# One core, four layers: an opening in another order, and modulation rows that come back from DRAM as turned columns

## The reference, cut to what matters

```python
c_act = jax.nn.silu(c)
for l in range(2):
    mod = c_act @ ada_w[l] + ada_b[l]              # 1024 -> 6 x 1024
    shift_m, scale_m, gate_m, shift_f, scale_f, gate_f = jnp.split(mod, 6, axis=-1)
    h = rms_norm(x, g_pre_mix[l]) * (1.0 + scale_m) + shift_m
    proj = h @ w_in[l] + b_in[l]
    q, k, v, u = jnp.split(proj, ...)               # q, k rotated by position
    attn_out = sliding_window_attention_with_sinks(q, k, v, sinks[l])
    pool_out = causal_pool_mixer(u, pool_w[l], pool_scale[l])
    mix = jnp.concatenate([attn_out, pool_out], -1) @ w_out[l]
    x = x + gate_m * rms_norm(mix, g_post_mix[l])
    h = rms_norm(x, g_pre_ffn[l]) * (1.0 + scale_f) + shift_f
    f = (jax.nn.silu(h @ w_gate[l]) * (h @ w_up[l])) @ w_down[l]
    x = x + gate_f * rms_norm(f, g_post_ffn[l])
```

## Time and profile before

| what | value |
|---|---|
| median of three runs | 1180.57 us (1179.1 to 1184.54) |
| the profiled execution, whole | 1183.38 us |
| its span, first to last instruction | 1181.3 us, mean granted PE clock 0.996 |
| PE busy | 1145.1 us, 97% |
| DVE busy | 808.8 us, 68% |
| ACT busy | 632.7 us, 54% |
| POOL busy | 28.3 us, 2% |
| chain that ended last | PE 78%, DVE 10%, DMA 7%, ACT 4% |

### The profile page before, as it was taken

One profiled execution on the slowest core, in us unless ns is written; L12 is line 12 of the kernel. 1 busy time (PEld: TensorE's weight loads), 2 busy tenths in 40 slices (PEclk: granted clock), 3 DMA queues, 4 the chain that ended last, 5 costly groups with the idle time before them and its releaser, 6 DMA issues.

```text
span 1181.3 us, 19635 instructions
## 1 busy us (share of the span) xinstructions
PE 1145.1 (97%) x7899; PEld 1025.8 (87%) x7899; DVE 808.8 (68%) x1255; ACT 632.7 (54%) x1114; POOL 28.3 (2%) x61
## 2 busy tenths in 40 slices
PE   5899999999989999999999999999999999999997
PEld 3466999999878999999898899999989889999996
DVE  5697966798996855554677668566666866766663
ACT  3066533355556644444755766455455676555543
POOL 3100000000000000010000000000000000000000
PEclk9999999999999999999999999999999999999999
DMA  9994899998435575585343455555534435555530
GB/s 380 410 421 196 323 280 299 291 393 322 175 131 192 215 273 207 216 254 201 126 148 145 172 205 181 185 188 194 176 119 161 172 112 198 194 180 197 191 107 36
DMA packets 37305, 252.97 MB, mean 214 GB/s; under 512 B 4416, under 2 KB 4704, under 8 KB 8928
## 3 DMA queue, kind: packets, MB, share of 16 engines
q1 hardware_dynamic: 34992, 244.47, 58.0%
q0 software_dynamic: 2080, 7.25, 1.7%
q10 hardware_dynamic: 144, 0.00, 0.0%
HBM read 250.64 MB, written 1.06 MB: 213 GB/s over the span
## 4 chain that ended last, share of the span: by engine, by line
PE 78%; DVE 10%; DMA 7%; ACT 4%; issue 2%; SPq 0%; DVEq 0%; ACTq 0%
PE bank L490 22%; PE bank L492 22%; PE bank L491 22%; DMA raw_w<-weights 7%; DVE lo_w L1576 3%; DVE raw_w L1586 3%; PE bank L497 3%; PE bank L586 2%; PE bank L539 2%; ACT gtok L1139 1%; PE bank L629 1%; ACT hi_w L1134 1%; PE bank L929 1%; ACT prob L1252 0%; PE bank L689 0%
## 5 line engine op out<-in xcount | busy, mean ns | idle before, releaser
L1576 DVE TENSOR_TENSOR lo_w<-raw_w,hi_w 128x1024 fp32r<-128x1024 f32 (+3 forms) x346 | 409.0, 1209 | 124.6 <-ACT hi_w L1134 124.2
L1134 ACT ACTIVATE hi_w<-raw_w 128x1024 fp32r<-128x1024 f32 (+3 forms) x346 | 350.1, 1040 | 151.1 <-DMA raw_w<-weights 83.5
L490 PE MATMUL bank<-in_hi,lo_w 128*128 128x256 f32 x1408 | 395.9, 281 | 0.0
L492 PE MATMUL bank<-in_hi,hi_w 128*128 128x256 f32 x1408 | 393.2, 279 | 0.0
L491 PE MATMUL bank<-in_lo,hi_w 128*128 128x256 f32 x1408 | 393.1, 279 | 0.0
L490 PEld LDWEIGHTS bank<-in_hi,lo_w 128*128 128x128 f32 x1408 | 264.2, 188 | 2.5 <-issue 0.8
L491 PEld LDWEIGHTS bank<-in_lo,hi_w 128*128 128x128 f32 x1408 | 263.7, 187 | 1.9 <-issue 0.5
L492 PEld LDWEIGHTS bank<-in_hi,hi_w 128*128 128x128 f32 x1408 | 264.6, 188 | 0.0
L490 PE MATMUL bank<-hi_w,hid_lo 128*128 128x512 f32 x352 | 139.7, 397 | 1.3 <-DVE hid_lo L2059 1.0
L492 PE MATMUL bank<-hi_w,hid_hi 128*128 128x512 f32 x352 | 139.0, 395 | 0.0
L491 PE MATMUL bank<-lo_w,hid_hi 128*128 128x512 f32 x352 | 139.0, 395 | 0.0
(11 more groups left out here) (218 smaller groups left out, 1142.8 us busy)
## 6 DMA issues: line engine op xcount, KB each, us to landing
raw_w<-weights SPq DMA_DIRECT2D x215, 1024.0 KB, 5.3
ink<-ink_w SPq DMA_DIRECT2D x8, 640.0 KB, 13.1
rows<-norm_rows POOLq DMA_DIRECT2D x5, 512.0 KB, 4.9
ink<-whole_w SPq DMA_DIRECT2D x2, 1024.0 KB, 23.5
early_out<-whole_w SPq DMA_DIRECT2D x2, 1024.0 KB, 12.8
rows<-mod_rows POOLq DMA_DIRECT2D x4, 512.0 KB, 9.1
raw_w<-weights SPq DMA_DIRECT2D x2, 832.0 KB, 4.4
const<-const_table SPq DMA_DIRECT2D x1, 1538.0 KB, 7.8
```

Source lines behind the costliest of these rows:

```text
L490: nc.tensor.matmul(o, st[1], mv[0], start=start, stop=False, **kw)
L492: return nc.tensor.matmul(o, st[0], mv[0], start=False, stop=stop, **kw)
L1134: nc.scalar.activation(hi_w[:, m % NSPLIT, cut], raw_view(unit)[:, cut], ACT.Identity).then_inc(*sig("hi_w", unit, i))
L1576: nc.vector.tensor_tensor(lo_w[:, m % NSPLIT, cut], raw_view(unit)[:, cut], hi_w[:, m % NSPLIT, cut].bitcast(F32), ALU.subtract).then_inc( ...
```

## The change

The opening sends c as one row of 4 KB ahead of x, and PE spreads it into two banks, from which ACT takes silu. The squares of T1 go to DVE, the norms stand ahead of the first `ada` products, T1's norm has a buffer of its own (`gained`), and the first two units come in halves. One of three ACT table loads on the way is gone.

`turn_column` turns a column `modcol` of 128 x 8 by one PE transpose into 8 x 128; `piece` on ACT copies that to `pieces`, and `row_out` writes it as 8 pieces of 512 bytes. This serves eight rows (`TURNED`), among them layer 0's gate and layer 1's gate, scale and shift, which were spread before. Layer 0's scale for the feed-forward is still spread, but ahead of `attention`; its shift stays in `ending`.

DVE's attention order of layer 0 is new: `ada(0, 8)` stands behind the first four evacuations, the other `ada` elsewhere among the softmax steps. ACT takes the pooled tiles at other places in both layers. In `whole_into_y` the loop over the two weight halves is the outer one. The bias row and pool weights of layer 1 load during layer 0's feed-forward.

```diff
-INK_AFTER = {("ada", 0, 0): (0,), ("ada", 0, 5): (1,), ("ada", 0, 1): (2,), ...
+INK_AFTER = {("ada", 0, 0): (1,), ("ada", 0, 1): (2,), ...
 def whole_into_y(u, T, before_last=None):
-                for c in range(2):
-                    for n in range(2):
-                        if (c, n) == (1, 1) and before_last is not None:
+                for n in range(2):
+                    for c in range(2):
+                        if (n, c) == (0, 1) and before_last is not None:
...
+                    if T == 1 and n == (0 if u == 1 else 1):
+                        done.then_inc(*sig("used_whole", u))
 def ending(L, w, one, other, front):
-                    spread_row(L, "scale", 1)
                     spread_row(L, "shift", 1)
+            def turn_column(L, kind, w):
+                pe.wait_ge(*due("modcol", L, kind, w))
+                job = ("column", L, kind, w)
+                b = take(job)
+                nc.tensor.transpose(b[0:KT, 0:P], modcol[:, ROWS[(L, kind, w)], :], k("ident")).then_inc(*sig(*job))
 def attention_windowed(L):    # PE
-                    banks(0, 1, *((4, 6, 5, 7) * 4))
+                    banks(0, 1, 4, 0, 1, *((6, 5, 7, 4) * 4))
...
                         turn_prob(n)
+                        if n == 3:
+                            turn_column(0, "gate", 0)
                         whole_into_y(u, T)
...
                     turn_prob(4)
+                    turn_prob(5)
                     into_y(1, 0, ("wo", 1, 2), 1, first=True)
-                    turn_prob(5)
-                    into_y(1, 0, ("wo", 1, 3), 1)
...
                 if L == 0:
-                    spread_row(L, "gate", 0)
-                for jp in range(2):
-                    attention(jp)
+                    spread_row(L, "scale", 1)
+                attention(0)
                 if L == 1:
-                    spread_row(L, "gate", 0)
-                    spread_row(L, "scale", 1)
-                    spread_row(L, "shift", 1)
+                    turn_column(1, "shift", 1)
+                attention(1)
+                if L == 1:
+                    into_y(1, 0, ("wo", 1, 3), 1)
 block.sync
+            sp.dma_start(c_row[0:1, :], a_c).then_inc(*sig("c_in", 0, by=16))
             sp.dma_start(x[:, :, :], a_x).then_inc(*sig("x_in", 0, by=16))
             sp.dma_start(const[:, 0:const_mid], a_const[:, 0:const_mid]).then_inc(*sig("const_in", 0, by=16))
-            sp.dma_start(c_row[:, :], a_c.to_broadcast([P, D])).then_inc(*sig("c_in", 0, by=16))
 row_out(L, kind, w)           # POOL
-                pool.wait_ge(*due("modcol", L, kind, w))
-                pool.dma_start(mod_rows[n, :].rearrange("(t p) -> p t", p=P), modcol[:, n, :], allow_slow_non_contiguous=True).then_inc(
+                pool.wait_ge(*due("piece", L, kind, w))
+                pool.dma_start(mod_rows[n, :].rearrange("(t p) -> t p", p=P), pieces[0:KT, TURNED.index((L, kind, w)) % 2, :]).then_inc(
...
             sinks_in(0)
-            pool.wait_ge(*due("tok", 0, 1, 2))
-            load(bias, a_bias[1:2, :], 1280, "bias_in", 1)
+            mod_row(0, "gate", 0)
 boundary(L, w, units)         # ACT
+                    rounded(0, 0)
+                    rounded(0, 1)
+                    y_squares(1, 0)
...
+            def piece(L, kind, w):
+                n = TURNED.index((L, kind, w))
+                if n >= 2:
+                    sc.wait_ge(*due("row_out", ROWS[TURNED[n - 2]]))
+                copy(("column", L, kind, w), pieces[0:KT, n % 2, :], ps(("column", L, kind, w))[0:KT, 0:P], "piece", L, kind, w)
 started()                     # ACT
-                sc.preload_act_table_set("natural_log_exp_and_others")
+                sc.preload_act_table_set("silu_and_others")
+                sc.wait_ge(*due("opening", "c", 1))
+                for c in range(2):
+                    nc.scalar.activation(c_row[:, cols(c)], ps(("opening", "c", c))[:, :], ACT.Silu).then_inc(...)
 attention_windowed(L)         # ACT
                     shares(4)
+                    piece(0, "gate", 0)
 gain(L, w, T, c)              # DVE
-                if w == 0:
-                    ve.wait_ge(*due("row", L, "gate", 0, c))
-                else:
-                    ve.wait_ge(*due("row0", L, "gate", 1))
+                ve.wait_ge(*due("row0", L, "gate", w))
 rest(T, c)                    # DVE
-                        ve.wait_ge(*due("y", 0, 0, 1, 1))
+                        ve.wait_ge(*(due("used_whole", 1) if c == 0 else due("y", 0, 0, 1, 1)))
 attention_windowed(L)         # DVE
-                    ada(0, 8)
                     ve.wait_ge(*due("rope1", 0))
                     ve.wait_ge(*due("bias_in", 0))
                     for c in range(2):
                         for T in range(2):
                             evacuate(0, T, c)
-                    ada(0, 9)
+                    ada(0, 8)
                     evacuate(0, 0, 2)
                     evacuate(0, 1, 2)
```

More of the change, by code:

```diff
@@ L542, in turn_norm @@
             def turn_norm(N, T, parts=(0, 1)):
+                src = gained if N == ("mix", 0) and T == 1 else normed
                 for c in parts:
                     pe.wait_ge(*due("normed", N, T, c))
-                    transposes(("tr", N, T, c), [normed[:, 512 * c + P * i:512 * c + P * (i + 1)] for i in range(4)])
+                    transposes(("tr", N, T, c), [src[:, 512 * c + P * i:512 * c + P * (i + 1)] for i in range(4)])
             def mixed_wait(L, unit):
@@ L965, in feed_forward @@
                 ending(L, 1, ("wd", L, WD - 2), ("wd", L, WD - 1), following)
+            pe.wait_ge(*due("ve_step", 1))
+            pe.wait_ge(*due("c_in", 0))
+            for c in range(2):
+                job = ("opening", "c", c)
+                nc.tensor.matmul(take(job)[:, :], tmp[0:1, 0:P], c_row[0:1, cols(c)], start=True, stop=True).then_inc(*sig(*job))
             pe.wait_ge(*due("const_in", 0))
-            pe.wait_ge(*due("vec_in", 0))
-            transposes(("vec",), [vrow[:, P * g:P * (g + 1)] for g in range(NVEC)])
             for T in range(2):
                 turn_norm(("mix", 0), T)
+            pe.wait_ge(*due("vec_in", 0))
+            transposes(("opening", "vec"), [vrow[:, P * g:P * (g + 1)] for g in range(NVEC)])
             for L in range(NL):
@@ L1093, in _ @@
             mod_row(1, "scale", 0)
+            load(bias, a_bias[1:2, :], 1280, "bias_in", 1)
+            pool.dma_start(poolw[:, 1, :, :], a_poolw[1].rearrange("g c d -> c g d")).then_inc(*sig("poolw_in", 1, by=16))
+            row_out(1, "gate", 0)
+            pool.wait_ge(*due("gained", "y", 0, 1, 1, 1))
+            row_back(1, "gate", 0)
             sinks_in(1)
+            row_out(1, "scale", 1)
+            row_back(1, "scale", 1)
+            mod_row(1, "shift", 1)
             pool.wait_ge(*due("normed", ("ffn", 1), 1, 1))
@@ L1583, in ada_tile @@
                     in_turn(unit)
+                if f == 0 and UNIT_NO[unit] < 2:
+                    ve.wait_ge(*due("ada_first", 1))
+                elif f == 0 or UNIT_NO[unit] < 2:
                     ve.wait_ge(*due(f"raw_w{UNIT_NO[unit] % NRAW}", unit))
@@ L1646, in scale @@
                     if T == 0:
-                        ve.wait_ge(*(due("row1", N[1], "scale", 0) if N[0] == "mix" else due("row", N[1], "scale", 1, c)))
+                        ve.wait_ge(*(due("row", 0, "scale", 1, c) if N == ("ffn", 0) else due("row1", N[1], "scale", 0 if N[0] == "mix" else 1)))
                     else:
```

146 lines of the change are left out of this document (81 added, 65 removed).

## The result

| | before | changed |
|---|---|---|
| median (4 runs each) | 1181.49 us (1179.1 to 1184.54) | 1171.12 us (1170.39 to 1172.02) |
| profiled execution, whole | 1183.38 | 1170.86 |
| its span | 1181.3 | 1168.9 |

The ratio of the times is 0.9911, with a 95% interval of 0.9889 to 0.9932. The change made the kernel 10.4 us faster; 13.5 was forecast, with a time of 1167.0 and a range of 1162 to 1178.

The account below looks back on a forecast made before the run. TensorE was taken to bound the kernel (78% of the chain, 97% busy). Layer 0's 7 plus layer 1's 7.3 minus 0.8 gave 13.5; 1180.6 - 13.5 = 1167, range 1162 to 1170, to 1178 with rival C and most of A.

Parts of the forecast that it names:

- rival C: Layer 0: the 1 MB units, not the opening, set its pace; it gains 2 instead of 7, time 1172; chance 0.14.
- part (a): Start up to layer 0's scores: opening 2.5 us earlier, scores at 53.9 instead of 58.16; 4.3 us won.
- Part (b): Scores to layer 0's first output: old stall and lower clock go, new stall of some 2.1 comes; 1.5 us won.
- part (c): Layer 0's ending: one spread fewer, stream 1.8 earlier, first feed-forward product at 102.0; 1.7 us won.
- The gate's row: Layer 0's gate by DRAM: lands at 90.7, ahead of the first gain at 93.4, so it costs nothing.
- Part (d): Layer 1's mixer: three spreads leave PE's path for two columns (5.1), idle shrinks (2.2); 7.3 us won.
- Part (e): Feed-forwards: five columns on PE at 0.15 each cost 0.8 us.
- A: Rows late in both mixers: way out stays at 12.6, gain only -2 to 2, time 1178 to 1183; chance 0.14.
- S: Layer 0: a queue delays both ways of the gate's row, some 1195, slower than before; chance 0.06.

Follow-up runs that it names:

- the earlier products: Changed kernel with each of adaLN's products 9 to 18 one place earlier in DVE's order: 1169.85 us.
- the early bias: The three edits, plus layer 0's bias row issued one adaLN product earlier (behind product 6, not 7): 1169.77 us.
- the three edits: Changed kernel with first two units whole, adaLN's products 9 to 18 one place earlier, layer 0's scores in free banks: 1168.92 us, ratio to before 0.9899.
- The other softmax order: Changed kernel, first two units whole, scores in free banks, adaLN's product 9 between first two softmax steps, 10, 11, 16 each behind two: 1172.76 us.

## Why the prediction was right or wrong

The time, 1171.12, lay in the whole range, but above the forecast's own part of it (1162 to 1170): of the cases it is rival C, "stream holds layer 0" with 1172, that came, not the likeliest one. C was right that a unit of the stream holds the first gain; its 1.8 of the stream did not come, so that its number fits so well is in part luck. How much earlier layer 0 reached four points, between the first profiles and between the second ones:

| up to | worked | first profiles | second profiles |
|---|---|---|---|
| the first score, part (a) | 4.3 | 2.4 | 0.5 |
| the end of y for T0, parts (a) and (b) | 5.8 | 3.3 | 1.4 |
| the first feed-forward product | 8.3 | 4.5 | 2.9 |
| the 200th split matmul, part (c) | 7.5 | 3.6 | 1.5 |

By size part (a) fell shortest; the mechanism that failed is in part (c).

**Part (a), 4.3, was mis-sized twice.** The change's own timing: the halves of the first two units cost the stream 1.07 against before, where I had booked 1.3 of c's bytes as won; so the bias was issued at 36.78 and not 35.5, landed at 46.34 and not 44.8, and scores started at 55.72 and not 53.9. With whole units they start at 53.71, as worked. And the yardstick: 58.16 stands 2.15 later than in the second profile of before, most of it by a lower clock that this one does not have. I counted its removal as a gain, and then took off 2.8 once more to come from the profiled execution to the median. The forecast from the same terms without that would have been 1169.

**Part (b), 1.5**: the fourth transposes wait for the shares as foreseen (1.41 instead of 2.1), and the clock did not fall behind that wait. y of T0 ended 3.3 earlier than before (first profiles) where 5.8 was worked; the 2.5 short are (a)'s 1.8 and 0.6 at the softmax. The 1.6 of lower clock behind the wait of 2.46, which this part counts as won, was rightly booked: it is in both profiles of before, and the changed kernel had the full clock there.

**Part (c), 1.7, is the step that failed.** "The stream comes 1.8 earlier" left out when the slots come free. The bytes would have allowed it: with the earlier products the unit lands at 89.60, 2.2 earlier than in before. I moved the products 9 to 17 in DVE's order without asking when each frees a slot, though the trace of before shows the chain: a unit is issued when the adaLN product of its slot is done. The unit landed at 93.90 instead of 90.0. The runs show what follows: first gain = landing of the first feed-forward unit + 3.46, in seven kernels (3.45 or 3.46, with landings from 90.5 to 100.5), and y's end where that is later (the early products, the early bias, and both kernels with the gate spread). The prediction had this wait, with 3.4, and got only its date wrong. The earlier products alone bring the first feed-forward product to 103.93, 1.9 of the 3.8 that it came behind the 102.0 worked; the three edits, which mend (a) as well, bring it to 102.48. From there to the 200th split matmul the changed kernel takes 29.0, before 28.1 and 27.7: I had taken off 0.8 for waits, and 1.0 to 1.4 came.

**The gate's row** was timely: 14.2 for the trip (14.5 worked), at 92.82 for a gain at 97.36. Its bytes cost the stream 1.2, as booked in (c). What I did not weigh is that in this kernel this is all that it saves: with the row spread the time is the same. POOL's two issues took 0.59 each, while DVE formed one adaLN product after the other. The Trainium skill, "SBUF — State Buffer", section "SBUF: two separate sides", says that GpSimd cannot write descriptors while VectorE runs a two-port operation. These issues show no such wait; no row tells whether DVE's products are operations of that kind.

**Part (d), 7.3**, right: 7.5 measured, 4.9 of it by the spreads and 2.6 by the rest, PE's waits for the most part, as the run with spreads tells apart. The shift's row landed at 367.39 and was used at 369.17, a margin of 1.8.

**Part (e), -0.8**: no such price is seen; that feed-forward takes 157.23, against 157.42 and 158.57, and 157.15 in the run with layer 1's spreads, which has one column less there: 0.1 for a column at the most. In before PE waits 0.27 and 1.28 us in this stretch, each time for DVE's `lo_w`, in the changed kernel not at all. Its three row writes of 1024 elements stand there: during the third, issued at 215.03, no unit lands between 218.60 and 228.24. That PE's waits come from these writes fits the rows, but no run tests it.

**Rivals**: A and S did not come. The way out took 5.0, not 12.6, and the way back 8.6, not 22.

**Open**: no run takes the new opening back by itself, so its share of layer 0's gain is not shown. Nor does a run move the first gains ahead of the unit's rounding and low part, which would part them from the stream.

## What to carry to other kernels

When work is reordered on an engine that also frees the buffers of a saturated stream, list for each unit when its slot comes free before and after, and take the dates, not the bytes. Before a stretch with a lowered clock is booked as a gain, look whether a second profile of the same kernel has it at the same work, not at the same microsecond, and do not correct to the median as well. Two limits that lie within a microsecond of each other eat single improvements; they show themselves by moving one at a time.

## What the runs showed of the hardware

A write of 1024 elements of 4 bytes to DRAM slowed the stream of weights while it lasted. These are windows of layer 0's feed-forward during a row's way out. In the kernel before:

```profile
149.00:152.00 3.00, 3.00 (x28) 3.00 (x27) 3.00 (x6) 1.87 (x3) 0.00 (x0) 1.00 0.89 30
```

In the changed kernel:

```profile
181.00:184.00 3.00, 3.00 (x27) 2.95 (x26) 3.00 (x5) 0.07 (x1) 0.51 (x1) 1.00 0.88 280
```

At the same share of busy DMA time, 0.9, one moves 30 GB/s and the other 280: a busy DMA is not one that moves data. The Trainium skill, "DMA: Bandwidth & Descriptors", section "Specifications", gives 512 bytes as the least transfer for full rate and says that below it a read-modify-write is made. The two windows and the 13.4 and 5.0 us of the two ways out agree with the limit; that a read-modify-write is the reason no run shows.

Two halves of a 1 MB unit, each 4 KB of every 8 KB of the source, and what loaded beside them moved at 260 GB/s between 6 and 9 us; with whole units it was 423 in the same microseconds.

Whether the clock falls behind a wait of PE cannot be told from the length of the wait alone (0.72 is a mean over its two levels, 1.2 and 2.4 GHz). Behind the 2.46 us both profiles of before had 0.72 of the clock over the next 6 us or so. Ahead of the scores the first had 0.72 over the 6 us behind its wait of 2.04 (from 50.58); the second has no such wait there and kept 1.00. The other softmax order fell to 0.72 behind 2.06, and the run with layer 1's spreads behind 1.69. But the three runs with a wait of 2.02 at the first transposes (the three edits, alone, with the spread and with the early bias) kept the full clock, and so did the run with whole units behind 2.33.
